# Overflow loop ahead of the experts, slot gates gathered from DRAM, one placed block instead of two

## The reference, cut to what matters

```python
g_logits = (hf @ w_group) + b_group
p_top, g_top = lax.top_k(jax.nn.softmax(g_logits, -1), 1)        # 1 of 4 groups
e_val, e_top = lax.top_k(e_logits, TOP_E)                        # 2 of its 8 experts
gate = jax.nn.softmax(e_val, -1) * p_top
expert = g_top * EXPERTS_PER_GROUP + e_top
...
hid = jax.nn.silu(xb @ w_gate[e]) * (xb @ w_up[e])               # 1024 -> 256
out = (hid @ w_down[e]) * buf_w[:, None]                         # 256 -> 1024, times the gate
...
x = x + hier_moe(rmsnorm(x, g_ffn), ...)
y = rmsnorm(x, g_final)
```

## Time and profile before

| | |
|---|---|
| median of 3 runs | 1221.99 us (1221.41 to 1223.98) |
| profiled execution | 1223.49 us, its span 1221.6 us |
| mean granted clock | 0.966 |
| PE busy | 1107.7 us, 91% |
| DVE busy | 629.3 us, 52% |
| ACT busy | 485.1 us, 40% |
| POOL busy | 205.7 us, 17% |
| packets of the weight queue q1 | 117332, 187.14 MB |

### The profile page before, as it was taken

The page is one execution under the profiler, slowest core; times in us unless marked ns, Lnnn a source line. Parts: engine busy times, 40 slices in busy tenths (PEclk is TensorE's granted clock), DMA queues, the critical chain, the costliest instruction groups (busy, mean ns, idle before and its releaser), DMA issues.

```text
span 1221.6 us, 19887 instructions
## 1 busy us (share of the span) xinstructions
PE 1107.7 (91%) x7589; PEld 792.5 (65%) x7589; DVE 629.3 (52%) x1650; ACT 485.1 (40%) x1033; POOL 205.7 (17%) x277
## 2 busy tenths in 40 slices
PE   5997799999999899999999899995799999999753
PEld 4984478787878898888988587884333333333242
DVE  6538978888888777543232652437331311212344
ACT  6447578787868334343433542210111111111112
POOL 1320023433342200000000000000011211111344
PEclk8999999999999999999999999997799999999976
DMA  8343173404030233432423805005899999999623
GB/s 285 45 96 52 33 257 153 113 2 113 1 89 2 59 104 92 113 96 81 119 62 87 301 15 224 36 35 207 327 391 418 419 418 418 419 418 416 241 103 155
DMA packets 129430, 214.20 MB, mean 175 GB/s; under 512 B 15041, under 2 KB 100449, under 8 KB 117044
## 3 DMA queue, kind: packets, MB, share of 16 engines
q1 hardware_dynamic: 117332, 187.14, 43.2%
q0 software_dynamic: 10272, 20.24, 4.9%
q10 hardware_dynamic: 1728, 5.51, 1.2%
HBM read 177.92 MB, written 38.57 MB: 177 GB/s over the span
## 4 chain that ended last, share of the span: by engine, by line
PE 73%; DVE 12%; ACT 5%; issue 4%; DMA 3%; POOL 2%; SPq 0%; DVEq 0%; POOLq 0%; ACTq 0%
PE psum L2646 13%; PE psum L2661 7%; PE psum L2361 5%; PE psum L2363 5%; PE psum L2362 5%; DVE place L1545 3%; PE psum L2333 2%; PE psum L2335 2%; PE psum L2334 2%; PE psum L2443 2%; PE psum L2512 2%; PE psum L2613 2%; PE psum L2513 2%; PE psum L2514 2%; PE psum L2417 2%
## 5 line engine op out<-in xcount | busy, mean ns | idle before, releaser
L2646 PE MATMUL psum<-place,place 128*32 128x512 f32 x1536 | 170.3, 595 | 1.2 <-issue 1.2
L1185 ACT ACTIVATE place<-place,place 128x768 uint8<-128x768 f32 (+3 forms) x128 | 125.5, 983 | 6.7 <-DVE place L1576 6.7
L2361 PE MATMUL psum<-place,place 128*128 128x512 f32 x288 | 121.9, 423 | 2.3 <-DVE place L1533 2.3
L2646 PEld LDWEIGHTS psum<-place,place 128*32 128x32 f32 x1536 | 49.1, 110 | 103.9 <-issue 101.5
L2363 PE MATMUL psum<-place,place 128*128 128x512 f32 x288 | 113.4, 394 | 0.0
L2362 PE MATMUL psum<-place,place 128*128 128x512 f32 x288 | 112.7, 391 | 0.0
L2661 PE MATMUL psum<-place,place 128*32 128x512 f32 x768 | 88.6, 602 | 2.3 <-DVE place L1985 2.3
L1991 DVE TENSOR_TENSOR place<-psum,place 128x256 f32<-128x256 f32 x24 | 10.2, 426 | 151.2 <-ACT place L1367 151.2
L2333 PE MATMUL psum<-place,place 128*128 128x256 f32 x288 | 85.7, 298 | 1.6 <-ACT place L1207 1.6
L2334 PE MATMUL psum<-place,place 128*128 128x256 f32 x288 | 82.1, 285 | 0.0
L2335 PE MATMUL psum<-place,place 128*128 128x256 f32 x288 | 82.0, 285 | 0.0
(11 more groups left out here) (341 smaller groups left out, 2498.8 us busy)
## 6 DMA issues: line engine op xcount, KB each, us to landing
place<-in_w_gate SPq DMA_DIRECT2D x32, 1024.0 KB, 13.5
place<-in_w_up SPq DMA_DIRECT2D x32, 1024.0 KB, 16.6
place<-in_w_down SPq DMA_DIRECT2D x32, 1024.0 KB, 13.1
place<-in_w_in SPq DMA_DIRECT2D x28, 512.0 KB, 6.4
expert_out<-place SPq DMA_DIRECT2D x1, 9216.0 KB, 28.5
place<-expert_out SPq DMA_DIRECT2D x9, 1024.0 KB, 13.4
place<-in_cache_attn_k SPq DMA_DIRECT2D x32, 256.0 KB, 3.2
place<-in_cache_attn_v SPq DMA_DIRECT2D x32, 256.0 KB, 3.5
```

Source lines behind the costliest of these rows:

```text
L1185: last = nc.scalar.activation(reached[j], score[j], ACT.Sign, bias=pivot.bitcast(F32)[:, j:j + 1], scale=-1.0, accum_out=minus[:, j - BY_A ...
L2361: nc.tensor.matmul(bank(4 + b), hT_hi[:, k, rows], hi, start=k == 0, stop=False)
L2646: last = nc.tensor.matmul(bank(b % 2)[rows], xT[b % 2][:, k, rows], w_gu[expert_of(b, q) % NSLOT][:, :, k, :], start=k == 0, stop=k == KD - 1)
```

## The change

There are four parts. First, the gates of the slots no longer come from a product: ScalarE writes the table of gates (128 x 18 numbers of 4 bytes) to DRAM (`gate_table`), and GpSimd gathers 128 gates for each block by the block's result rows, in groups of four blocks (`gates_of`) that stand behind gather(2) to gather(7). Second, the tables and the product for overflow blocks, and the overflow loop itself, stand ahead of the blocks inside one branch that every engine skips when the count is zero; for that SyncE, GpSimd, ScalarE, TensorE and VectorE each load the count once it is known (`counted`). Third, block 22 is scattered like the others, and block 23 alone is placed by TensorE. Fourth, the last sums are divided anew: GpSimd sums tiles 1 to 5 instead of 1 to 7, tile 7 joins those that `put_sum` adds, and down(23) writes two other banks.

```diff
-NOVER, TOGETHER = 24, 6
+NOVER = 24
...
-PLACED = (NMAIN - 2, NMAIN - 1)
+PLACED = (NMAIN - 1,)
 NSENT = NMAIN - len(PLACED)
-SUM_ON_PE, SUM_ON_POOL, SCALE_ON_ACT = (1, 3, 5), (1, 2, 3, 4, 5, 6, 7), (2, 4, 6)
+SUM_ON_PE, SUM_ON_POOL, SCALE_ON_ACT = (1, 3, 5, 7), (1, 2, 3, 4, 5), (2, 4, 6)
...
+        gate_table = nc.dram_tensor("gate_table", (2 * NTOK, 1), F32).ap()
...
+        def gate_landed(b):
+
+            return pair_in[b // 4 % 2], 32 * 6 + 64 * (b // 8) + 64
...
-            return bank((2, 4, 0, 6)[t % 4], start, width)
+            return bank((0, 4, 6, 2)[t % 4], start, width)
+
+        def down_bank(b, half_n):
+
+            return bank((2 if b + 1 == NMAIN else 6) + half_n)
+
+        counted, tables_set, frames_set = ((slots_done, n + 1) for n in range(3))
+        gates_out = (x_three_in, 16 + 16)
...
                 elif not BEFORE_FRAMES[e]:
-                    sp.wait_ge(frames_ps, len(PARTS) + 1)
+                    sp.wait_ge(frames_ps, len(PARTS))
...
+            sp.wait_ge(*counted)
+            n_over = sp.value_load(over_meta[0:1, NOVER:NOVER + 1], min_val=0, max_val=NOVER)
+            with sp.If(0 < n_over):
+                sp.wait_ge(*tables_set)
+                with sp.Fori(0, NOVER) as i:
+                    with sp.If(i < n_over):
+                        e = sp.value_load(over_meta[0:1, bass.ds(i, 1)], min_val=0, max_val=NE - 1)
+                        w_g, w_u, w_d = (i_[n][0, bass.ds(e, 1)] for n in ("w_gate", "w_up", "w_down"))
+                        sp.dma_start(w_gu_over[:, 0], w_g.rearrange("a (p k) n -> p (a k) n", k=KD)).then_inc(w_over_in, 16)
+                        sp.dma_start(w_gu_over[:, 1], w_u.rearrange("a (p k) n -> p (a k) n", k=KD)).then_inc(w_over_in, 16)
+                        sp.dma_start(w_dn_over, w_d.rearrange("a (p k) n -> p (a k) n", k=2)).then_inc(w_over_in, 16)
+                        sp.wait_ge(over_out, 16 * i + 16)
+                        stand(sp)
...
+            def gates_of(group):
+                if group >= 2:
+                    pool.wait_ge(*gate_landed(4 * group - 8))
+                for b in range(4 * group, 4 * group + 4):
+                    pool.indirect_dma_start(slot_gate[:, b:b + 1], None, gate_table, bass.IndirectOffsetOnAxis(ap=block_rows[:, b:b + 1], axis=0),
+                                            bounds_check=2 * NTOK - 1, oob_is_err=False).then_inc(gate_landed(b)[0], 16)
+
+            pool.memset(slot_gate, 0.0).then_inc(pool_set, 1)
             gather(0)
             gather(1)
             pool.wait_ge(frames_done, 2)
             pool.wait_ge(*zeroed)
+            pool.wait_ge(pool_set, 5)
+
+            pool.wait_ge(*counted)
+            n_over = pool.value_load(over_meta[0:1, NOVER:NOVER + 1], min_val=0, max_val=NOVER)
...
             for b in range(2, NSENT + 5):
                 if b < NMAIN:
                     gather(b)
+                if b == 2:
+                    pool.wait_ge(*gates_out)
+                if b - 2 < NMAIN // 4:
+                    gates_of(b - 2)
                 if b >= 5:
                     scatter(b - 5)
...
-                if b == 0:
-                    act.wait_ge(frames_done, 4)
+                act.wait_ge(*gate_landed(b))
...
+            act.dma_start(gate_table.rearrange("(j t p) a -> p j (t a)", j=2, p=P), gates, allow_slow_non_contiguous=True).then_inc(gates_out[0], 16)
+
+            act.wait_ge(*counted)
+            n_over = act.value_load(over_meta[0:1, NOVER:NOVER + 1], min_val=0, max_val=NOVER)
+            with act.If(0 < n_over):
+                with act.Fori(0, NOVER) as i:
...
+            def over_count():
+
                 L(v, tt(e_cnt, bank(5, 0, NE), C("base"), ALU.subtract))
                 L(v, tt(t_thr, e_cnt.unsqueeze(2).broadcast_to([P, NE, 9]), C("thr").unsqueeze(1).broadcast_to([P, NE, 9]), ALU.is_gt))
                 L(v, nc.vector.reduce_sum(e_blk, t_thr, AX))
                 L(v, nc.vector.tensor_tensor_scan(e_incl, e_blk, e_blk, 0.0, ALU.add, ALU.max))
+                nc.vector.tensor_copy(over_meta[:, NOVER:NOVER + 1], e_incl[:, NE - 1:NE]).then_inc(slots_done, 1)
+                v.wait_ge(*counted)
...
+            over_count()
+            all_gates()
+            n_over = v.value_load(over_meta[0:1, NOVER:NOVER + 1], min_val=0, max_val=NOVER)
+            with v.If(0 < n_over):
+                over_links = Order(sd_done, STEPS)
+                over_slots(over_links.link)
+                over_blocks(over_links.link)
+                ...
...
+            v.wait_ge(h2_out[0], 16 * ((T + 1) // 2))
+            v.wait_ge(h2_out[1], 16 * (T // 2))
+            rows_second(0)
+            rows_second(1)
             for b in range(NMAIN):
                 hidden(b)
-                if b == 1:
-                    gates_of_slots()
+                if b + 1 == NMAIN:
+                    hidden_turned(b)
                 if b >= 1 and b - 1 in PLACED:
                     rows_low(PLACED.index(b - 1))
                 elif b >= 1:
                     rows_out(b - 1)
                 if b + 2 < NMAIN:
                     rows_second(b + 2)
-                hidden_turned(b)
-                if b == 1:
-                    over_blocks()
+                if b + 1 < NMAIN:
+                    hidden_turned(b)
                 if b - 2 >= NSLOT and b - 2 - NSLOT < len(PLACED):
                     places(b - 2 - NSLOT)
...
-            n_over = v.value_load(over_meta[0:1, NOVER:NOVER + 1], min_val=0, max_val=NOVER)
-            with v.Fori(0, NOVER // TOGETHER) as r:
-                with v.If(TOGETHER * r < n_over):
...
-            def over_frames():
-
-                pe.wait_ge(rows_done, len(PARTS))
-                pe.wait_ge(slots_done, 1)
-                for j in range(2):
-                    for t in range(T):
-                        last = nc.tensor.matmul(bank(5, 0, NOVER + 2 * NMAIN), at_row(j, t), at_tables[:, j, t, :], start=j == t == 0, stop=j == 1 and t == T - 1)
-                last.then_inc(frames_ps, 1)
...
+                if 1 <= b < NMAIN - 1:
                     pe.wait_ge(y_act, b)
                     pe.wait_ge(y_dve, b)
                 for half_n in range(2):
                     for k in range(2):
                         for q in range(PARTS_OF):
                             rows = slice(ROWS * q, ROWS * q + ROWS)
-                            last = nc.tensor.matmul(bank(6 + half_n)[rows], hidT[b % 2][:, k, rows],
+                            last = nc.tensor.matmul(down_bank(b, half_n)[rows], hidT[b % 2][:, k, rows],
                                                     w_dn[expert_of(b, q) % NSLOT][:, k, 512 * half_n:512 * half_n + 512],
...
+            n_over = pe.value_load(over_meta[0:1, NOVER:NOVER + 1], min_val=0, max_val=NOVER)
+            with pe.If(0 < n_over):
+                pe.wait_ge(*tables_set)
+                for j in range(2):
+                    for t in range(T):
+                        last = nc.tensor.matmul(bank(5, 0, NOVER), at_row(j, t), at_over[:, j, t, :], start=j == t == 0, stop=j == 1 and t == T - 1)
+                last.then_inc(ov_frames[0], 1)
...
-                    over_frames()
             down(NMAIN - 1)
-            pe.wait_ge(y_act, NMAIN)
-            pe.wait_ge(y_dve, NMAIN)
-            n_over = pe.value_load(over_meta[0:1, NOVER:NOVER + 1], min_val=0, max_val=NOVER)
-            with pe.Fori(0, NOVER // TOGETHER) as r:
...
+                if n == 0 and t == 3:
+                    pe.wait_ge(y_act, NMAIN)
+                    pe.wait_ge(y_dve, NMAIN)
...
```

More of the change, by code:

```diff
@@ L417, in build @@
         y_rows = [take(D) for _ in range(2)]
-        at_tables = place(y_at, 2 * T * (NOVER + 2 * NMAIN), "p (j t n) -> p j t n", F32R, j=2, t=T)
-        frames_now = take(1).bitcast(I32)
+        at_over = place(y_at, 2 * T * NOVER, "p (j t n) -> p j t n", F32R, j=2, t=T)
+        frames_now, rows_now = (take(1).bitcast(I32) for _ in range(2))
+        over_gate = take(1)
         placed_at = [take_rounded(NTOK, "p (t n) -> p t n", t=T) for _ in PLACED]
@@ L435, in build @@
         top[0] = up_at[0] + 2 * KD * DE + D
-        line = take(P + 2 * T)
+        line = take(P + T)
         line_columns, line_tiles = line[:, 0:P], line[:, P:]
-        frame_f, tile_frames = take(1), take(2 * T)
+        frame_f, tile_frames = take(1), take(T)
         assert top[0] <= mark_h
-        top[0] = up_at[1]
-        x_over = take(D)
-        over_at = take(2 * NTOK, "p (n c) -> p n c", n=2 * T)
-        assert top[0] <= up_at[1] + 2 * KD * DE
-        y_over = place(dn_at[1], D)
+        over_at = up_at[3]
+        w_gu_over, w_dn_over = up(up_at[4]), dn(over_at)
+        x_over, y_over = place(over_at + 2 * D, D), place(over_at + 3 * D, D)
+        assert over_at + 4 * D <= AT_ROWS
         back_to(mark)
@@ L1435, in _ @@
         def _(v):
-            order = Order()
+            order = Order(dve)
             def mean_square(t):
@@ L2066, in over_slots @@
```

(37 more changed lines are left out.)

190 lines of the change are left out of this document (62 added, 128 removed).

## The result

The changed kernel takes 1230.65 us (median of 5 runs, 1229.82 to 1232.31) against 1221.99 us before (5 runs, 1218.74 to 1224.41): 1.0065 times as long, interval 1.0048 to 1.0082. It is slower by 8.7 us, where 1219.5 was forecast, and lies above the range. Its profiled execution has a span of 1230.0 us.

A forecast was written before the change was run, and what follows sets the result against it. Blocks 1 to 22 were taken as bound by TensorE and DMA alike, so only front and end could move: +9.7 and −12.0 give −2.3 us from 1221.99, 1219.7, forecast as 1219.5, range 1204.5 to 1228.5.

The forecast's parts named there:

- the first rival on the other side: Gate table's write misses the gap in weight traffic, so further weights come between: 1229 us, chance 14%.
- the gap: Pause in weight loads, 883.4 to 886.5 us, about 3 us, into which the table's write was to fit.
- The prediction's own signs of being wrong: Write landing before 865 or after 890, or down(22) to the span's end outside 57 to 66 us.
- One for one: On the DMA engines, one 4-byte gate packet passes per weight packet, so one each 0.31 us.
- The early landing: Rival: engines take a dozen or so small writes per turn, table there by about 863; 1206 us, chance 20%.
- The landing: When the gate table's write to DRAM lands: about 886 us, after the weight queue runs dry at 883.4.
- The stall: TensorE idle 11.5 us awaiting gather(3) after down(0), +9.0 against before; half clock then adds 2.0, vanished gaps give −1.3.
- The end: Stretch behind down(22): loop gone, later read-back, fewer VectorE waits, 4 taken back; −12.0 us, bounds −3.8 to −16.
- The first step: Behind down(22): 10.1 us of loop gone, 6.3 back as later read-back; −3.8 us up to rows_low of block 23.
- x: The end of down(22), from which the forecast counts the times of the kernel's end.
- the late case: The table misses the gap in weight traffic: 1229 us, chance 14%; the range left half of it out.
- the main case: Table lands at about 886, stall 8 to 12 us, end −16 to −8: 1214 to 1225 us, chance 60%.

The follow-up runs named there:

- the version that keeps the gains: Changed kernel with the table written in 72-byte pieces, blocks 22 and 23 both placed, and gates gathered in groups of two: 1207.21 us, 0.9867 of the time before.
- the kernel with the outer branch: Kernel before, its overflow loop put inside one branch on the count being over zero, still behind the blocks: 1218.49 us, ratio 0.9975.
- the kernel with the wait moved: Changed kernel with GpSimd's table wait and first gate gathers moved from behind gather(2) to behind gather(4): 1226.32 us, ratio 1.0040.

## Why the prediction was wrong

The mechanism of the forecast was the right one: the write of 4-byte pieces takes turns with the weights, GpSimd waits for it, gather(3) is queued behind, TensorE stalls and then runs at half clock, and a shorter end pays part of it back. The sign came out wrong because two terms of the sum were mis-sized, by 5.8 us in front and 4.9 behind. In number it is the case of the first rival on the other side (1229, for a table that misses the gap), but not its course: the table did make the gap. The prediction's own signs of being wrong both came: the write landed after 890 (890.8), and the end lay outside 57 to 66 us (66.1).

**One for one: right.** From 859 to 876 us, by queue (packets, MB, share of 16 engines):

```profile
q1 hardware_dynamic: 769, 5.63, 83.3%
q0 software_dynamic: 368, 1.10, 16.3%
q10 hardware_dynamic: 764, 0.00, 2.5%
```

q10 is the table's queue: 764 packets beside 769 of the weights. This was the forecast, from the earlier trace rows. The Trainium skill ("DMA: Bandwidth & Descriptors", section "Queues, rings and completion order") has an engine drain a whole packet of some 9 to 17 descriptors before it changes queues. If the records are descriptors, this trace doesn't agree: 764 beside 769. The early landing that the rule would give didn't come.

**The landing: 886 forecast, 890.8 measured.** Three pieces of this term failed. The weights thin out at 885.8 instead of 883.4; the whole stage is 0.8 to 1.4 us later, which is about half of that, and the other half stays unexplained. Then the rest of the table takes 1.7 us instead of 0.6. Its first packet starts at 858.9, 3.8 us behind the issue and not at once, so more is left; and it doesn't go at 9.3 ns a piece:

```profile
DMA packets 412, 0.07 MB, mean 67 GB/s; under 512 B 404, under 2 KB 404, under 8 KB 404
...
q10 hardware_dynamic: 400, 0.00, 22.5%
```

400 packets in 1 us (886 to 887) on 16 engines are 25 an engine, on average one each 40 ns, though they keep an engine busy for 22.5% of the time only, 9 ns each. In the earlier trace rows I had multiplied the small packets' count by their busy share; the share says how long a packet is worked on, and the spacing is another number, which the same window would have given: 1316 packets in 1.5 us on 16 engines are one each 18 ns. Last, the signal came 3.2 us behind the last packet (887.5), where I had allowed 2. The three pieces are 2.4, 1.1 and 1.2 us.

**The stall: +9.0 forecast for the fourth transposes, +13.9 measured** (902.92 against 888.99). 4.8 of the difference are the landing. GpSimd took 1.0 us from the landing to its first gather, then 1.30 a gather, and gather(3) landed in 5.8: 12.1 from table to frames against 12.0 forecast. The restart cost 2.2 against 2.0, the later gaps gave back 0.6 rather than 1.3. gate_up(1) came only 0.8 us earlier (877.73 against 878.48), not 2.5; counted from the first transposes (862.60 against 861.22) it is 2.1. With no gates this start came 1.2 us sooner after the first transposes, gate_up(0) having taken 8.7 us there instead of 7.6, and F gained 0.4 in all. So this term is worth 0.4 to 2 us. In gate_up(0) the granted clock was 0.80 there and 0.93 before; why it rose later was not tried.

**The end: −12.0 forecast, −7.1 measured.** The first step held: read-back at x + 5.7 to x + 6.1 (6.0), rows_low over at x + 14.5 (14.8). From there on the waits of VectorE come out right in total: from its sums of tiles 1 and 2 to its last instruction they are 13.4 us where they were 22.8, 9.4 less, and the forecast had −8.6 − 4.8 + 4.0 = −9.4. That is partly luck. The waits for sums of GpSimd shrank by 5.0 us (3.38, 1.57 and 7.01 to 1.33, 2.25 and 3.37), not by 8.6; those for TensorE by 5.2; and those for GpSimd's powers grew by 0.8, where 4.0 had been taken back. Two steps failed outright. VectorE's work was taken to be as quick as before: the whole stretch but its waits is 31.1 us against 26.9, where +1.2 was forecast. Two of its sums, of 3.36 us at 1183.25 and 2.25 at 1206.91 instead of 1.22, make up these 3 us; what held them up was not tried. And the price of 25 more indirect transfers at the end was put at nothing: from ScalarE's last store to the end of the span are 7.0 us against 4.9, which is GpSimd's DRAIN. All the kernels that gather gates have the 7 us, and all without have 5.0, the one with the new division of sums and no gates among them.

**The parts of the end, as the runs separate them.** Without the loop: −11.4 (73.2 to 61.8; forecast 10.1 of "issue"). Everything else but the scatter of block 22: −6.0 (to 55.8). In this are the new division of sums and banks and the 2 us of the DRAIN, so the division gains about 8; no run has it alone. Scattering block 22: +10.2 (to 66.0). The forecast booked the last as +6.3 for the later read-back and then −4.8 for the second placed block; the +6.3 was too small, since the chain of sums hangs on the read-back from tile 0 on, and the −4.8 was no gain at all: with two placed blocks and no loop VectorE waits 1.1 us for TensorE in these sums. So the part of the change that scatters block 22 costs 10 us by itself.

**The chances.** 0.25 stood on slower. The range ended at 1228.5 because half of the late case was cut off, and the main case's own range (1214 to 1225) let the stall be 8 to 12 us and the end −16 to −8. The stall came out at 14.7 and the end at −7.1: both lie outside their bounds, on the dear side.

## What to carry to other kernels

Count the pieces of a transfer, not its bytes: beside a busy queue each piece costs a turn, so 9 KB in 2304 pieces landed after 35.7 us and in 128 pieces after 8.5. Before one engine waits for a transfer, look at what else is queued behind the wait; moving the wait down the queue helps only as far as the next consumer, which here stood 8 us on. Price an edit's parts one at a time: this one held gains of 11 us and about 8, and losses of 15, 10 and 2, and the version that keeps the gains takes 1207 us. It still pays the 2 us of GpSimd's DRAIN; whether the gates could come without indirect transfers was not tried.

## What the runs showed of the hardware

**Each indirect transfer of GpSimd made its closing DRAIN 0.08 us longer.** 6.65 us after 46, 8.69 after 71, in ten kernels without an exception; here the execution ends with it.

**One branch of TensorE took 6 us.** The branch over the loop's body took 6.04 and 6.08 us behind the blocks, and 0.24 us ahead of them. Ahead of them TensorE is idle until gather(0) has landed, so a wait right behind the branch wouldn't show. The length of the jump alone doesn't make it: of the four branches over the same body in the earlier trace rows the first took 6.08 and the other three 0.22 to 0.23. In both long ones a packet of 16 KB of an instruction queue is under way (1155.4 to 1161.5 in the kernel with the outer branch):

```profile
q8 instruction: 1, 0.02, 1.1%
```

It ends at 1164.6 and at 1160.1, and the branch 1.4 us later in both. That fits a wait for code that has to be fetched beside the read-back loads, but no run separates it.

**Groups of four gathers came with late signals of TensorE.** In the kernel with the wait moved, gate_up(3)'s last product starts at 916.05; ScalarE, which waits for it alone, starts at 918.94:

```profile
918.94 0.39 ACT L1399 ACTIVATE place<-psum 128x256 f32<-128x256 f32 x1 [8.91 <-remote]
...
931.39 0.39 ACT L1399 ACTIVATE place<-psum 128x256 f32<-128x256 f32 x1 [8.92 <-remote]
```

In blocks without such a group the distance is 0.7 us. It happened four times in each of four kernels with groups of four (2.7 to 4.0 us), each time while GpSimd was at the last gathers of a group or at the scatter behind it. Two of the 16 are in block 0, where no scatter stands behind the group yet. It happened in none of the kernels with groups of two or without gathers of gates. The changed kernel has groups of four too and shows no such delay, so the count alone is not the condition. What holds the signals up stays open, and so does whether the groups cause it.

**Times spread more than one part's worth.** The same kernel before took 1216.8 to 1227.7 in 25 runs. Effects of 3 us are told here from intervals, and from F and E, not from single runs.
